# One run of attention over eight heads, begun before the SSM and convolution outputs are scaled and turned

## Time and profile before

| | us |
|---|---|
| median of 3 runs | 1274.85 |
| lowest, highest | 1273.84, 1284.81 |
| the profiled execution | 1278.19 |
| its span | 1276.4 |
| PE, DVE, ACT, POOL busy in it | 1144.3, 971.0, 715.4, 363.8 |

### The profile page before, as it was taken

The page is one execution under the profiler, slowest core; times in us unless marked ns, Lnnn a source line. Parts: engine busy times, 40 slices in busy tenths (PEclk is TensorE's granted clock), DMA queues, the critical chain, the costliest instruction groups (busy, mean ns, idle before and its releaser), DMA issues.

```text
span 1276.4 us, 16422 instructions
## 1 busy us (share of the span) xinstructions
PE 1144.3 (90%) x5604; PEld 898.4 (70%) x5604; DVE 971.0 (76%) x1152; ACT 715.4 (56%) x859; POOL 363.8 (29%) x341
## 2 busy tenths in 40 slices
PE   5899988759889899996699999999999999999992
PEld 3447565548677678786578888888877877787771
DVE  1979998545455665367689999998988998898871
ACT  5511225754444562221477777777777777777751
POOL 2313014435626000011223232332333433334221
PEclk9999989979999999997699999999999999999996
DMA  6700010030002000326399999999999999999940
GB/s 202 159 1 1 0 17 10 2 131 2 0 0 99 0 34 1 116 102 276 104 426 384 371 395 380 395 393 377 377 368 376 367 353 364 367 352 369 356 138 10
DMA packets 55475, 260.80 MB, mean 204 GB/s; under 512 B 31088, under 2 KB 31760, under 8 KB 41616
## 3 DMA queue, kind: packets, MB, share of 16 engines
q1 hardware_dynamic: 45344, 243.03, 49.6%
q0 software_dynamic: 10096, 17.34, 5.6%
HBM read 252.25 MB, written 26.35 MB: 218 GB/s over the span
## 4 chain that ended last, share of the span: by engine, by line
PE 57%; DVE 16%; DMA 15%; ACT 5%; issue 4%; SPq 2%; POOL 0%; DVEq 0%; ACTq 0%; POOLq 0%
PE psum L2071 23%; DMA w<-in_w 13%; PE psum L2091 8%; PE psum L1986 6%; DVE arena L1303 5%; PE psum L1912 5%; PE psum L1946 4%; DVE arena L1105 4%; PE psum L1932 3%; PE psum L1747 2%; DMA out<-arena 2%; PE psum L1898 1%; PE psum L2061 1%; DVE xgT_rest L1630 1%; DVE am L1436 1%
## 5 line engine op out<-in xcount | busy, mean ns | idle before, releaser
L1637 DVE TENSOR_TENSOR w_rest<-w,w_high 128x2048 fp32r<-128x2048 f32 x136 | 305.1, 2285 | 20.4 <-ACT w_high L1027 19.9
L1027 ACT ACTIVATE w_high<-w 128x2048 fp32r<-128x2048 f32 x136 | 256.3, 1912 | 97.0 <-DMA w<-in_w 66.1
L2071 PE MATMUL psum<-w_high,xgT_high 128*128 128x512 f32 x544 | 218.2, 401 | 17.7 <-DVE xgT_rest L1630 17.6
L2071 PE MATMUL psum<-w_rest,xgT_high 128*128 128x512 f32 x544 | 213.7, 393 | 0.0
L2071 PE MATMUL psum<-w_high,xgT_rest 128*128 128x512 f32 x544 | 213.3, 392 | 0.0
L1644 DVE TENSOR_TENSOR w_rest<-w,w_high 128x2048 fp32r<-128x2048 f32 x68 | 152.4, 2282 | 1.8 <-ACT w_high L1037 1.8
L1037 ACT ACTIVATE w_high<-w 128x2048 fp32r<-128x2048 f32 x68 | 126.4, 1908 | 28.3 <-DMA w<-in_w 28.1
L2071 PEld LDWEIGHTS psum<-w_high,xgT_high 128*128 128x128 f32 x544 | 102.8, 189 | 44.9 <-issue 20.6
L660 POOL DMA_INDIRECT out<-arena,idx x34 | 93.8, 2758 | 112.0 <-DVE arena L1657 108.8
L2071 PEld LDWEIGHTS psum<-w_rest,xgT_high 128*128 128x128 f32 x544 | 102.9, 189 | 22.0
L2071 PEld LDWEIGHTS psum<-w_high,xgT_rest 128*128 128x128 f32 x544 | 103.2, 190 | 20.2
(11 more groups left out here) (266 smaller groups left out, 2059.9 us busy)
## 6 DMA issues: line engine op xcount, KB each, us to landing
w<-in_w SPq DMA_DIRECT2D x102, 2048.0 KB, 19.9
arena<-in_x SPq DMA_DIRECT2D x5, 1024.0 KB, 6.2
h_scratch<-arena SPq DMA_DIRECT2D x8, 512.0 KB, 2.6
out<-arena SPq DMA_DIRECT2D x8, 512.0 KB, 3.6
arena<-in_x SPq DMA_DIRECT2D x1, 3072.0 KB, 9.8
arena<-in_w_in SPq DMA_DIRECT2D x1, 2688.0 KB, 15.0
arena<-in_w_in SPq DMA_DIRECT2D x1, 2048.0 KB, 12.3
wout_y_raw<-in_w_out SPq DMA_DIRECT2D x1, 2048.0 KB, 7.8
```

Of the source, the lines that this page charges most:

```text
L1027: act.activation(w13h[k][:, c, :], w13[b][k][:, c, :], ACT.Copy).then_inc(W13H_READY[k], 1)
L1637: dve.tensor_tensor(w13l[b][k][:, c, :], w13[b][k][:, c, :], w13h[k][:, c, :].bitcast(F32), S_).then_inc(W13_SPLIT[k], 1)
L2071: last = pe.matmul(psum[:, k, :], x_[:, c, :], w_[:, c, :], start=(c == 0 and n == 0), stop=(c == KC - 1 and n == 2))
```

## The change

It changes, between the latent projections and the output projection:

- `project_qkv` of tiles 0 to 2 stands ahead of the convolution's turn, tiles 3 to 7 right behind it; ScalarE saves all eight ahead of the silu. `sum_qk(1)` stands ahead of the layer norm. ScalarE's square root for `qks` stands ahead of the copies of the turned SSM output.
- VectorE makes head 0 alone, GpSimd heads 1 to 7.
- The loop over passes is gone: 64 steps are written out with constant counts. The tiles come as 7, 6, 1, 0, 5, 4, 3, 2.
- Q and K of the next head are turned in four parts at steps 1 to 4 of a head (`turn_head`), all through PSUM bank 7.
- Values are made for two steps at once (`values(m)`, at odd steps), V as the weights, the two tiles in the lower and upper 64 partitions of bank 6. The result is copied (`save_ohT`), turned back (`turn_values`) in the next step and scaled (`save_o`).
- Squaring, scaling and turning of the two outputs are cut into pieces of one tile (`y_step`, `turn_y`): the convolution is squared in the steps of head 0, the SSM in head 1, scaled in heads 2 and 3, turned in 8 pieces at steps 29 to 32 and 37 to 40. The gate product is in step 3 (`gate_ssm`). GpSimd's two RMS follow its head 4.
- The output projection begins right after the last values; their turning follows its first tile.
- The SSM, gate and convolution buffers are moved in SBUF; some semaphores are joined.

```
-        STEPS = 2 * NT
-        tile_of = [(NT - 1 - n % NT // 2) if n % 2 == 0 else n % NT // 2 for n in range(STEPS)]
+        STEPS = H * NT
+        ORDER = [i for k in range(NT // 4) for i in (NT - 1 - 2 * k, NT - 2 - 2 * k, 2 * k + 1, 2 * k)]
+        tile_of = [ORDER[n % NT] for n in range(STEPS)]
+        PAIRS = STEPS // 2
...
+        Y_PIECE_AT = {STEPS - 2 * NT + n: k for k, n in enumerate((1, 2, 4, 6, 8, 10, 11, 12))}
+        HEAD_BANK = 7
+        CONV_SQUARE_AT, SSM_SQUARE_AT, CONV_SCALE_AT, SSM_SCALE_AT = (range(NT * h, NT * (h + 1)) for h in range(4))
+        Y_TURN_AT = {NT * (3 + k // 4) + 5 + k % 4: k for k in range(NT)}
+        def next_part(n):
+            return (n // NT + 1, n % NT - 1) if n // NT + 1 < H and 1 <= n % NT <= 4 else None
...
 SP
-            sp.wait_ge(mid_done, 1)
+            sp.wait_ge(y_saved, NT)
             w_out_c = w_out[0].rearrange("(c p) n -> p c n", p=P)
...
 GpSimd
+            pool.wait_ge(qk_scaled, 1)
+            for h in range(1, H):
+                if h >= 2:
+                    pool.wait_ge(k_turned, 2 * h - 2)
+                    pool.wait_ge(q_turned, 2 * h - 2)
+                for a in range(2):
+                    make_heads_part(pool, hlink, settle, h, h % 2, a, rot)
+                pool.sem_inc(heads_made, 1)
+                if h == 4:
+                    pool.wait_ge(mid_squared, 1)
+                    rms(64, 72, CW, NT, EPS, mid_rms)
+                    pool.wait_ge(mid_squared, 2)
+                    rms(48, 56, SW, NT, EPS, mid_rms)
...
 ScalarE
+            for n in range(STEPS):
+                for f in range(first_fill[n], first_fill[n + 1]):
+                    if not by_dve[f]:
+                        act.wait_ge(pT_filled, f + 1)
+                        w = min(4, tile_of[n] + 1 - 4 * (f - first_fill[n]))
+                        if f >= 4:
+                            act.wait_ge(pv_done, pair_of[f - 4] + 1)
...
+                if n + 2 < STEPS:
+                    exponentials(n + 2)
+                if next_part(n):
+                    h, part = next_part(n)
+                    if part % 2 == 0:
+                        save_kT(h, part // 2)
+                y_step(n)
+                if n in Y_PIECE_AT:
+                    high_y_piece(Y_PIECE_AT[n])
...
 VectorE
+            dve.sem_inc(qk_scaled, 1)
+            for a in range(2):
+                make_heads_part(dve, link, None, 0, 0, a, rot_dve)
+            dve.sem_inc(head0_made, 1)
...
+                if n % 2 == 0 and n >= 2:
+                    save_o(n // 2 - 1)
+                if n + 2 < STEPS:
+                    row_max(n + 2)
+                if next_part(n):
+                    h, part = next_part(n)
+                    if part % 2 == 1:
+                        save_qT(h, part // 2)
+                if n % 2 == 1:
+                    save_ohT(n // 2)
+                if n == 3:
+                    gate_ssm()
+                if n - 1 in Y_PIECE_AT:
+                    rest_y_piece(Y_PIECE_AT[n - 1])
...
 TensorE
+            for i in range(3):
+                project_qkv(i)
             pe.wait_ge(conv_done, 1)
             turn(lambda i, c: cperm[:, c, i, :], R_CONV)
-            for i in range(5):
+            for i in range(3, NT):
                 project_qkv(i)
...
+            def values(m):
+                if m >= 1:
+                    pe.wait_ge(o_saved, 2 * m)
+                h, tiles = 2 * m // NT, tile_of[2 * m:2 * m + 2]
+                saved(first_fill[2 * m + 2] - 1)
+                for j in range(tiles[0] + 1):
+                    for k in range(2):
+                        if j <= tiles[k]:
+                            last = pe.matmul(psum[k * VD:(k + 1) * VD, 6, 0:P], vtok[:, j, h * VD:(h + 1) * VD],
+                                             probT[(first_fill[2 * m + k] + j // 4) % 4][:, j % 4, :],
+                                             start=(j == 0), stop=(j == tiles[k]))
+                last.then_inc(pv_done, 1)
+            def turn_values(m):
+                pe.wait_ge(ohT_saved, m + 1)
+                pe.transpose(psum[:, 6, P:2 * P], ohT[m % 2], ident[:, :]).then_inc(otok_filled, 1)
+            for part in range(4):
+                turn_head(0, part)
+            scores(0)
+            scores(1)
+            pe.wait_ge(hi_drained, R_GLU + 1)
+            for n in range(STEPS):
+                turn_probs(n)
+                if n % 2 == 0 and n >= 2:
+                    turn_values(n // 2 - 1)
+                if n + 2 < STEPS:
+                    scores(n + 2)
+                if next_part(n):
+                    turn_head(*next_part(n))
+                if n in Y_TURN_AT:
+                    turn_y(Y_TURN_AT[n])
+                if n % 2 == 1:
+                    values(n // 2)
...
                 project_out(i, (yTh, yTl), (wYh, wYl), y_out_filled)
+                if i == 0:
+                    turn_values(PAIRS - 1)
+                    pe.wait_ge(o_saved, H * NT)
                 turn_o(i)
```

More of the change, by code:

```diff
@@ L246, in build @@
         bns = sb("bns", [P, NT, 8])
+        ohT = [at(OHT0 + P * b, P) for b in range(2)]
         psum = ctx.enter_context(nc.psum_tensor("psum", [P, 8, 512], F32))
@@ L326, in build @@
         FILLS = first_fill[STEPS]
+        pair_of = [n // 2 for n in range(STEPS) for _ in range(fills_of[n])]
         by_dve = [f % 3 == 2 for f in range(FILLS)]
@@ L837, in save_qkv @@
                 act.sem_inc(qk_saved, 1)
-            for i in range(5):
+            for i in range(NT):
                 save_qkv(i)
@@ L1375, in _ @@
             dve.sem_inc(ln_done, 1)
[L1376 to L1378 removed]
+            dve.wait_ge(scratch_in, 16)
             kp2 = at(14336 + 2560, NT, RD)
@@ new lines, in turn_head @@
+            def turn_head(h, part):
+                k, a = part // 2, 1 - part % 2
+                buf, turned = (qn, kn)[a][h % 2], (q_turned, k_turned)[a]
+                if part == 0:
+                    if h == 0:
+                        pe.wait_ge(head0_made, 1)
+                    else:
+                        pe.wait_ge(heads_made, h)
+                if h >= 1:
+                    if a == 1:
+                        pe.wait_ge(qT_saved, 2 * h + k)
+                    else:
+                        pe.wait_ge(kT_saved, 2 * h + k + 1)
+                if h == 0 and part == 0:
+                    pe.wait_ge(lo_drained, F_QKV(NT - 1, 3) + 1)
+                if part == 0 and h - 1 in (4, 5):
+                    pe.wait_ge(y_saved, 4 * (h - 4))
+                bank = HEAD_BANK if h else part
+                for i in range(4 * k, 4 * k + 4):
+                    last = pe.transpose(psum[0:QH, bank, (i % 4) * P:(i % 4 + 1) * P], buf[:, i, :], ident[:, :])
+                last.then_inc(turned, 1)
@@ new lines, in scores @@
+            def scores(n):
+                h, i = n // NT, tile_of[n]
+                if n % NT == 0:
+                    pe.wait_ge(qT_saved, 2 * h + 2)
+                    pe.wait_ge(kT_saved, 2 * h + 2)
+                if n >= 2:
+                    pe.wait_ge(p_ready, n - 1)
+                L = (i + 1) * P
+                for k in range((L + 511) // 512):
+                    w = min(512, L - 512 * k)
+                    last = pe.matmul(psum[:, 2 * (n % 2) + k, 0:w], qT[h % 2][0:QH, i * P:(i + 1) * P], kT[h % 2][0:QH, 512 * k:512 * k + w],
+                                     start=True, stop=True)
+                last.then_inc(s_filled, 1)
```

395 lines of the change are left out of this document (154 added, 241 removed).

## The result

| | before | after |
|---|---|---|
| median of 4 runs, us | 1276.26 | 1264.14 |
| lowest, highest | 1273.84, 1284.81 | 1260.49, 1265.04 |
| the profiled execution | 1278.19 | 1263.85 |
| first turned probabilities | 283.28 | 267.19 |
| output projection begins | 470.25 | 458.78 |

The medians of the table differ by 12 us, where 26 was forecast, and their ratio is 0.9905. The measured ratio is 0.986 (95%: 0.981 to 0.991).

A forecast was written before the change was run, and what follows sets the result against it. Attention was taken as bound by TensorE plus each pass's restart, after a relay of waits. The profiled 1278.19 us minus 21.8 (start) and 4 (attention) gives 1252.4; the median being 3.3 lower, the forecast is 1249, range 1231 to 1266.

The forecast's parts named there:

- likeliest case: The forecast case: start gains 21.8 us, attention 4, total 1249, own range 1241 to 1259; chance 0.55.
- I take 254, between the ends: Start: VectorE's head 0 is made at 254, between 250 undisturbed and 256.5 slowed by GpSimd building head 1.
- third rival: Start: square root blocks ScalarE, gate matmuls partly at 1.2 GHz, GpSimd holds head 0; 10 us lost, 1264; chance 0.10.
- eight bare heads with mode changes, last one shorter: Attention: 166 us for eight heads, plus 3 for changes between value forms, minus 5 for the last head.
- squares and gate product: Attention steps: ScalarE's squares cost 2.2 us for each of heads 0 and 1, the gate product at step 3 2.5.
- scalings, wait for RMS: Attention steps: scalings cost 1.7 us for each of heads 2 and 3, ScalarE's wait at step 16 for GpSimd's RMS 1.
- turns of y: Attention steps: 8 pieces of 4 turns with a 0.5 copy cost 2 us.
- y pieces: Attention's end: eight y pieces on ScalarE and VectorE cost 3 us for each of the last two heads.
- walk: Attention: one head followed through three in-order queues; TensorE waits 2.25 us, 20.8 per head, 166 for eight.
- first rival: Attention stays TensorE-bound as waits overlap: a head is 20 us, attention 160 to 170, total 1231; chance 0.25.
- Half-width values that don't overlap: Attention values: the half-width form saves nothing, 3.2 x 8 = 26 us come back, total 1274; chance 0.05.
- Steps in series: Attention's odd steps: no stage of one pair overlaps the next, about 27.5 us per head, total 1282; chance 0.05.

The follow-up runs named there:

- the run with head 0 alone: The changed kernel, with GpSimd starting head 1 only when VectorE has made head 0; 1259.18 us, ratio 0.983.
- left-out scaling: The changed kernel without the convolution and SSM outputs' squares and scalings on ScalarE and GpSimd's two RMS; 1373.52 us, total not comparable.
- pieces earlier: The changed kernel, with half of w_out loaded behind the gate product and the y pieces in heads 5 and 6; 1262.91 us, ratio 0.986.
- RMS early: The changed kernel, with GpSimd's RMS of the convolution output behind its head 3 in place of head 4; 1261.70 us, ratio 0.985.
- the old form: The changed kernel, with values again made with probabilities as weights, one tile after the other, without turn back or its copy; 1298.09 us, ratio 1.0125.
- the kernel with all four edits: The changed kernel with GpSimd waiting for head 0, zT copies before the square root, convolution finished ahead of attention, y pieces earlier; 1253.76 us, ratio 0.977.

## Why the forecast was right in kind and short in size

The direction and the likeliest case's mechanism held, and the range held by 2 us (1264.14 in 1231 to 1266). The likeliest case's own range, 1241 to 1259, did not, and 1264 lies above the 1262 under which the forecast put 0.84. Two terms of the sum are off.

**The start: "I take 254, between the ends".** This step failed. The choice between 250 and 256.5 took a value between two prices without a reason for it, and the price was the upper one and a little more: head 0 was made at 258.03. The upper end came from 1024-wide products at 2.37 for 1.23, a factor of 1.93, and over the whole head that factor is nearly right: 14.5 for 7.3 is 2.0. Only within the head is it uneven: the 256-wide product went from 0.42 to 1.91, the first one stayed at 0.96. So head 0 is 4.0 of the 5.7 us by which the gain missed 21.8 (16.1 also lies under its 19 to 26), and the head turns at a lower clock (3.44 for 16 against 1.91 in the run with head 0 alone) are 1.5. The times ahead of head 0 stood (the last sum forecast at 240, measured 239.97; scaled 243, measured 243.3). With GpSimd held back the first probabilities came at 261.70, where the forecast had 261.5, but this agreement is luck: head 0 ended 2.5 us before the forecast's 254, and the gate matmuls, which the forecast let end by 252, ended at 253.47. The third rival (10 us of 21.8 go, 1264) named the square root, the gate matmuls at the lower clock and head 0. That its total is what was measured is luck too: the start lost 5.7 and not 10, the gate matmuls' 9.37 cost nothing, since head 0 ended after them, and attention did not give nothing, it cost 4.6.

**Attention: 183 forecast, 191.6 measured.** The forecast did not fit together here: its list of heads (23, 23, 22.5, 22, 21, 21, 24, 19) adds up to 175.5, its terms to 183.3. Read as bare heads and loads:

| term | forecast | measured | shown by |
|---|---|---|---|
| eight bare heads with mode changes, last one shorter | 166 + 3 - 5 | 172 - 2.7 | left-out scaling; pieces earlier |
| squares and gate product | 6.9 | 4.9 | heads 0 and 1 less 21.5 each |
| scalings, wait for RMS | 4.4 | 7.1 | heads 2 and 3; RMS early |
| turns of y | 2 | 4.7 | heads 3 to 5 with the scalings left out, less 21.5 each |
| y pieces | 6 | 5.6 | heads 6 and 7, less 21.5 and 18.8 |

A bare head at 21.5 for 21.2 (20.8 and the mode changes) looks like a sound walk, but two misses cancel in it: TensorE is busy 20.2 us in such a head (ends are modelled in this), where the forecast had 18.55 and 0.4 for the mode changes, and it waits 1.3, where the walk had 2.25. The first rival, heads of 20, had the waits right at 1.3 and the work wrong. A part of the missing work is the turn back of the values: step by step against the old form (head 1 of both) the values themselves save 3.2 as forecast, and the turns back cost 0.9 for 0.4. The rest of it stays open.

The wait for the RMS was forecast at 1 and cost 4.0. The walk did find its place and its cause (GpSimd's head 4 in front of it), and its 15 us for GpSimd was right (306.19 to 321.04); but ScalarE stood at step 16 after 12.3 us and not after 14, and the clock behind the wait had no price. The last head's "minus 5" was 2.7: without scores to fill it, TensorE waits there for copies instead (1.78 us ahead of its first values). The turns of y cost 0.6 a piece wherever they stand (1.7, 2.4 and 0.6 over a bare head for three, four and one piece in heads 3, 4 and 5), where the sum had 0.25. That is less than its own price for four turns, 0.44, and they are most of it: in head 4 TensorE's busy time rises by 2.0 of the 2.4 (22.24 against 20.20).

**The clock.** The forecast had 1.00 in attention. It was 0.93 and 0.94 in the two heads in which TensorE waited longest in one place (2.02 in head 0, 2.86 in head 2), and 1.4 us of busy time each hang on that. Nearly 3 of the 8.6 us are of this kind. Such a wait does not decide it by its length: see the last section.

**The other rivals.** Half-width values that don't overlap are ruled out by 1.96 us for 30 records. Steps in series aren't seen: no head reached the 27.5 of that rival, the longest took 26.75. The queues passed on SP cost nothing, as forecast: the two halves of `w_out` moved in head 5 (0.83 DMA share), and no row of TensorE waits for them there.

Open: why the part behind attention scatters; how much of a stalled head's clock is chance (next section but one); where the rest of TensorE's busy time in a bare head comes from; why head 6 took 2.1 us more with the pieces at other steps; and why the gate matmuls took 8.86 in four kernels and 7.17 in a fifth, all after 2.15 or 2.16 of idle time.

## What to carry to other kernels

Work laid into the steps of a pipelined stage is paid by the step in which the bound engine waits for it, and by the clock behind that wait. Price it as a wait in a place, not as the busy time of an idle engine. An engine with real idle time (GpSimd, here at 5.2 and 4.5 us for what VectorE does in 1.27 and 2.28) is the cheaper place when its answer is wanted late. Work for which an engine is idle ahead of the stage needn't go into it: the convolution's squares and scalings, put back ahead of attention into ScalarE's wait, cost the start 0.8 us and gave attention 9, or 6.5 against the run with head 0 alone. Where two engines' products overlap on the critical path, hold the one that isn't wanted first: one changed wait gave back 5.5 us of the start.

## What the runs showed of the hardware

- A 256-wide VectorE product beside GpSimd's 768-wide one took 1.91 us for 0.42, up to 0.28 behind the end of the other; a chain of 13 products took 14.5 for 7.3. GpSimd's own 768-wide product went from 1.81 to 2.40.
- A wait of TensorE of 2.0 to 2.9 us in the midst of attention was followed by the lower clock (part of the head at 1.2 GHz in place of 2.4) in the changed kernel's heads 0 and 2, and cost 1.4 to 1.6 us beside itself. It isn't certain to come: in the kernel with all four edits a wait of 2.18 in the same place left the clock at 1.00, and its head took 23.2 in place of 25.7 with the wait at 2.50. Nor does it need a long wait: in the last head the 30 records took 1.93 behind a wait of 1.78 in the changed kernel and 3.32 behind one of 1.79 with head 0 alone, and its 22 records took 1.50 or, with the scalings left out, 2.79, both behind a wait of 1.09.
- Full-width value records in the old form brought stretches (heads) with a clock of 0.64 to 0.88 that the half-width form, in the same order of steps, did not have.
